# Rope tables beside w_out, operand parts freed tile by tile, norm columns inside blocks and out of the banks' turn

## The reference, cut to what matters

```
u = rmsnorm(x) @ w_in;  y = [pool_mixer(u), ssm_mixer(u)]          # first block
x = x + y @ w_out                                                  # "mix"
x = x + (silu(rmsnorm(x) @ w_gate) * (rmsnorm(x) @ w_up)) @ w_down # "ffn"
x = rmsnorm(x)                                                     # norm_final, end of the first block
cos, sin = rope_tables(positions)                                  # second block
z = rmsnorm(x) @ w_in_2          # "z": latents of q and kv, k_pe, 7 x 256 RWKV columns, then gates
y_a = mla_branch(z, cos, sin);  y_b = rwkv7_branch(z)              # "wkv", "qkv", attention, scan
x = x + (gate_a * y_a + gate_b * y_b) @ w_out_2                    # "mix2"
x = x + square(relu(rmsnorm(x) @ w_ffn_up)) @ w_ffn_down           # "ffn2"
x = x + sigmoid(rmsnorm(x) @ w_ple_gate) * (p @ w_ple_proj)        # "ple"
out = rmsnorm(x)
```

## Time and profile before

| | us |
|---|---|
| median of 3 runs (3169.36 to 3174.61) | 3171.29 |
| the profiled execution, its own time | 3166.37 |
| its span, first to last instruction | 3164.5 |
| TensorE busy in it | 2930.0 |
| VectorE / ScalarE / GpSimd busy | 1429.1 / 752.2 / 388.6 |

### The profile page before, as it was taken

The page is one execution under the profiler, slowest core; times in us unless marked ns, Lnnn a source line. Parts: engine busy times, 40 slices in busy tenths (PEclk is TensorE's granted clock), DMA queues, the critical chain, the costliest instruction groups (busy, mean ns, idle before and its releaser), DMA issues.

```text
span 3164.5 us, 38694 instructions
## 1 busy us (share of the span) xinstructions
PE 2930.0 (93%) x16576; PEld 2391.8 (76%) x16576; DVE 1429.1 (45%) x2068; ACT 752.2 (24%) x1010; POOL 388.6 (12%) x293
## 2 busy tenths in 40 slices
PE   5879899999999999988888879989999999999998
PEld 4757678888888877866667657768878888888876
DVE  6983433332333554434442655674343333333354
ACT  4133211111111321024332423231221111111232
POOL 0000101000010210000000700122221101111221
PEclk7989999999999999999989989889999999999999
DMA  4051011111111123234436321325211111111111
GB/s 153 32 123 40 35 56 49 54 40 54 54 40 54 52 76 111 80 124 127 130 119 176 87 54 55 107 95 186 85 38 52 54 40 54 54 40 54 53 54 54
DMA packets 222442, 236.97 MB, mean 75 GB/s; under 512 B 60256, under 2 KB 174816, under 8 KB 221376
## 3 DMA queue, kind: packets, MB, share of 16 engines
q1 hardware_dynamic: 222272, 234.49, 23.2%
HBM read 178.50 MB, written 56.20 MB: 74 GB/s over the span
## 4 chain that ended last, share of the span: by engine, by line
PE 80%; DVE 12%; ACT 3%; issue 2%; DMA 2%; SPq 1%; POOL 0%; DVEq 0%; ACTq 0%
PE bank L618 19%; PE bank L619 19%; PE bank L620 19%; PE bank L2407 2%; PE bank L1761 2%; PE bank L2427 2%; PE bank L1762 2%; PE bank L1763 1%; PE bank L2605 1%; PE bank L3119 1%; PE bank L3121 1%; PE bank L3120 1%; PE bank L3128 1%; DVE w_lo L182 1%; DVE gates L182 1%
## 5 line engine op out<-in xcount | busy, mean ns | idle before, releaser
L618 PE MATMUL bank<-op_hi,w_hi 128*128 128x512 f32 x1824 | 716.4, 393 | 35.3 <-DVE gates L182 14.4
L619 PE MATMUL bank<-op_lo,w_hi 128*128 128x512 f32 x1824 | 713.9, 391 | 0.0
L620 PE MATMUL bank<-op_hi,w_lo 128*128 128x512 f32 x1824 | 713.6, 391 | 0.0
L618 PEld LDWEIGHTS bank<-op_hi,w_hi 128*128 128x128 f32 x1824 | 345.4, 189 | 111.1 <-issue 31.2
L620 PEld LDWEIGHTS bank<-op_hi,w_lo 128*128 128x128 f32 x1824 | 345.0, 189 | 72.3
L619 PEld LDWEIGHTS bank<-op_lo,w_hi 128*128 128x128 f32 x1824 | 345.4, 189 | 71.4
L182 DVE TENSOR_TENSOR w_lo<-w_raw,w_hi 128x2048 fp32r<-128x2048 f32 (+2 forms) x116 | 256.3, 2210 | 209.0 <-ACT w_hi L423 205.2
L618 PE MATMUL bank<-f_hi,w_hi 128*128 128x512 f32 x864 | 336.7, 390 | 3.2 <-POOL f_lo L182 3.2
L619 PE MATMUL bank<-f_lo,w_hi 128*128 128x512 f32 x864 | 336.8, 390 | 0.0
L620 PE MATMUL bank<-f_hi,w_lo 128*128 128x512 f32 x864 | 336.8, 390 | 0.0
L182 DVE TENSOR_TENSOR hT<-hT,bank 128x512 f32<-128x512 f32 x256 | 169.7, 684 | 326.3 <-PE bank L620 326.0
(11 more groups left out here) (454 smaller groups left out, 3966.4 us busy)
## 6 DMA issues: line engine op xcount, KB each, us to landing
record<-record_scratch SPq DMA_DIRECT2D x16, 1024.0 KB, 5.3
w_raw<-in_w_ffn_up SPq DMA_DIRECT2D x16, 1024.0 KB, 5.2
w_raw<-in_w_ffn_down SPq DMA_DIRECT2D x16, 1024.0 KB, 4.8
w_raw<-in_w_in SPq DMA_DIRECT2D x13, 1024.0 KB, 5.5
w_raw<-in_w_gate SPq DMA_DIRECT2D x11, 1024.0 KB, 4.9
w_raw<-in_w_up SPq DMA_DIRECT2D x11, 1024.0 KB, 5.0
w_raw<-in_w_down SPq DMA_DIRECT2D x10, 1024.0 KB, 4.8
w_raw<-in_w_in SPq DMA_DIRECT2D x17, 512.0 KB, 4.2
```

The costliest lines, as they stand in the source:

```text
L618: t.matmul(ps[:], hi[:, k, wc], x[0][:, k, xc], start=k == 0, stop=False)
L619: t.matmul(ps[:], hi[:, k, wc], x[1][:, (k + turn) % KD, xc], start=False, stop=False)
L620: last = t.matmul(ps[:], lo[:, k, wc], x[0][:, k, xc], start=False, stop=k == kt - 1)
```

## The change

1. `dense` gets an order of its k and a signal `free`: behind the last block of w_out (and of w_out_2) each k counts up, so that ScalarE and VectorE write part k of the next operand while that block still runs. The first block of w_out takes k in the order 4 to 7, 0 to 3. The last two residual tiles and their squares move behind the first parts.
2. The rope tables are computed in w_out's second block; the load of the positions and the two stores move ahead in SP's queue. VectorE's wait for the stores stays where it was.
3. The columns and spreads of norms no longer take a turn of the banks (`ahead`): they use the next ones, and the next block starts at its own.
4. The sum of squares for norm_mix_2 moves from GpSimd to VectorE, and the last tile's squares of both norms are no longer added but multiplied by the ones themselves (32 products instead of 16).
5. The norms of the latents move into the first two RWKV blocks, columns ahead of k = 2 and spread ahead of k = 6.

```diff
-        b = order[self.turn[group] % len(order)]
-        self.turn[group] += 1
+        b = order[(self.turn[group] + (ahead or 0)) % len(order)]
+        self.turn[group] += ahead is None
...
+                if free and j + 4 >= len(jobs):
+                    if n < kt - 1:
+                        last.then_inc(*T.up(free, k))
+                    else:
+                        T.also(free, k)
...
-            ps = tile_of(t, "all", name, half)
+            ps = tile_of(t, "all", name, half, ahead=1 + half)
...
-        ps = tile_of(t, "all", name)
+        ps = tile_of(t, "all", name, ahead=0)
...
     def mix_sync(q):
-        for i in range(5):
+        for i in range(3):
+            wt1.load_at(q, i)
+            if i == 1:
+                q.wait_ge(*Sm.T.of("pooled", 3, 1))
+                q.wait_ge(*Sm.V.of("glu lo", 7, 1))
+                q.dma_start(mem.pos[:], a["positions_2"].to_broadcast([P, L])).then_inc(*d_pos.up(by=16))
+        rope_sync(q)
+        for i in range(3, 5):
             wt1.load_at(q, i)
...
-        s.wait_ge(*wt1.used(B_OUT + 3))
         for k in range(KD):
+            s.wait_ge(*T.of("op", k))
             if k >= 6:
                 s.wait_ge(*Sm.V.of("h", k, 1))
...
-            if k in (2, 3):
-                s.wait_ge(*Sm.V.of("h", k + 4, 1))
-                nm1.square(s, k + 4, hT[:, k + 4, :])
+            if k >= 6:
+                nm1.square(s, k, hT[:, k, :])
...
         for b in range(4):
             wt1.lo_at(v, B_OUT + b)
+            if b == 1:
+                yield from rope_vector(v)
...
         for k in range(KD):
-            if 1 <= k <= 2:
-                yield from residual_vector(v, Sm, "out", hT, (5 + k,), "h")
+            if k == 3:
+                yield from residual_vector(v, Sm, "out", hT, (6, 7), "h")
+            v.wait_ge(*T.of("op", (k + 4) % KD))
...
-    nm_h = Norm("norm_mix_2", Sf, mem.sq, mem.acc, Sf.G)
+    nm_h = Norm("norm_mix_2", Sf, mem.sq, mem.acc, Sf.V)
...
         for n, nm in enumerate((nm_h, nm_x)):
+            t.wait_ge(*Sf.V.of(nm.name, "sum", KD - 2))
+            t.wait_ge(*Sf.A.of(nm.name, "sq", KD - 1))
             for j in range(L // P):
-                last = t.matmul(ps[:, 8 * n + j:8 * n + j + 1], nm.acc[:, j * P:(j + 1) * P], ones[:, 0:1], start=True,
-                                stop=True)
+                for m, x in enumerate((nm.acc, nm.sq[(KD - 1) % 2])):
+                    last = t.matmul(ps[:, 8 * n + j:8 * n + j + 1], x[:, j * P:(j + 1) * P], ones[:, 0:1], start=m == 0,
+                                    stop=m == 1)
...
                     if i > 1:
+                        nm_h.add(v, i - 1)
                         nm_x.add(v, i - 1)
                     yield
-        nm_x.add(v, KD - 1)
...
-        for n in range(1, KD):
-            nm_h.add(g, n)
-            yield
...
+        norm_q = {2: lambda: columns_tensor(t, T, nm_q, "cols q", Sz.G.of("latent_q", "sum", 2)),
+                  6: lambda: spread_tensor(t, T, ncol[:, 0, :], "rs q", Sz.V.of("col q"))}
+        norm_kv = {2: lambda: columns_tensor(t, T, nm_kv, "cols kv", Sz.G.of("latent_kv", "sum", 1)),
+                   6: lambda: spread_tensor(t, T, ncol[:, 0, :], "rs kv", Sz.V.of("col kv"))}
...
         for b, n in enumerate(rwkv_blocks):
-            yield from block(B_RWKV + b, "rwkv", n)
-            if b == 0:
-                columns_tensor(t, T, nm_kv, "cols kv", Sz.G.of("latent_kv", "sum", 1))
-                spread_tensor(t, T, ncol[:, 0, :], "rs kv", Sz.V.of("col kv"))
+            yield from block(B_RWKV + b, "rwkv", n, (norm_q, norm_kv)[b] if b < 2 else None)
```

More of the change, by code:

```diff
@@ L134, in begin, with open @@
         self.turn, self.tenant, self.opened = dict.fromkeys(self.groups, 0), {}, set()
-    def open(self, group, *label):
+    def open(self, group, *label, ahead=None):
         assert label not in self.opened, label
@@ L591, in after, with tile_of @@
                 e.wait_ge(*s.total())
-    def tile_of(t, group, *label):
-        ps = psum.open(group, *label)
+    def tile_of(t, group, *label, ahead=None):
+        ps = psum.open(group, *label, ahead=ahead)
         for w in psum.free(*label):
@@ L602, in landed, with dense @@
             e.wait_ge(*d.total())
-    def dense(t, T, w, i, x, kt, jobs, ready, group="all", turn=0, at=None):
+    def dense(t, T, w, i, x, kt, jobs, ready, group="all", turn=0, at=None, order=None, free=None):
         hi, lo = w.view(w.hi, i), w.view(w.lo, i)
@@ L611, in dense @@
             tiles = [tile_of(t, group, *label) for _, _, label in four]
-            for k in range(kt):
+            for n, k in enumerate(order or range(kt)):
                 if j == 0 and at is not None and k in at:
@@ L617, in dense @@
                 for (wc, xc, label), ps in zip(four, tiles):
-                    t.matmul(ps[:], hi[:, k, wc], x[0][:, k, xc], start=k == 0, stop=False)
+                    t.matmul(ps[:], hi[:, k, wc], x[0][:, k, xc], start=n == 0, stop=False)
                     t.matmul(ps[:], hi[:, k, wc], x[1][:, (k + turn) % KD, xc], start=False, stop=False)
-                    last = t.matmul(ps[:], lo[:, k, wc], x[0][:, k, xc], start=False, stop=k == kt - 1)
-                    if k == kt - 1:
+                    last = t.matmul(ps[:], lo[:, k, wc], x[0][:, k, xc], start=False, stop=n == kt - 1)
+                    if n == kt - 1:
                         last.then_inc(*T.up(*label))
+                if free and j + 4 >= len(jobs):
[3 more added lines that the diff above has]
+                        T.also(free, k)
             yield 11
@@ L1253, in mix_tensor @@
             yield from dense(t, T, wt1, B_OUT + b, op, KD, halves_of([(0, 2 * b), (P, 2 * b + 1)], "out"),
-                             (lambda k: Sm.V.of("pool lo" if k < 4 else "glu lo", k, 1)) if b == 0 else None, turn=4)
+                             (lambda k: Sm.V.of("pool lo" if k < 4 else "glu lo", k, 1)) if b == 0 else None, turn=4,
+                             order=(4, 5, 6, 7, 0, 1, 2, 3) if b == 0 else None, free="op" if b == 3 else None)
     def mix_scalar(s):
@@ L1276, in mix_scalar @@
             wt1.hi_at(s, B_OUT + b)
+            if b == 1:
+                yield from rope_scalar(s)
             for i in (2 * b, 2 * b + 1) if b < 3 else ():
@@ L1420, in norm_h_tensor @@
     def norm_h_tensor(t):
-        ps = tile_of(t, "all", "cols h")
-        t.wait_ge(*Sf.V.of("norm_final", "sum", KD - 1))
-        t.wait_ge(*Sf.G.of("norm_mix_2", "sum", KD - 1))
+        ps = tile_of(t, "all", "cols h", ahead=0)
         for n, nm in enumerate((nm_h, nm_x)):
+            t.wait_ge(*Sf.V.of(nm.name, "sum", KD - 2))
+            t.wait_ge(*Sf.A.of(nm.name, "sq", KD - 1))
             for j in range(L // P):
-                last = t.matmul(ps[:, 8 * n + j:8 * n + j + 1], nm.acc[:, j * P:(j + 1) * P], ones[:, 0:1], start=True,
-                                stop=True)
+                for m, x in enumerate((nm.acc, nm.sq[(KD - 1) % 2])):
+                    last = t.matmul(ps[:, 8 * n + j:8 * n + j + 1], x[:, j * P:(j + 1) * P], ones[:, 0:1], start=m == 0,
+                                    stop=m == 1)
         last.then_inc(*Sf.T.up("cols h"))
@@ L2927, in mix2_vector @@
         for k in range(KD):
-            if 1 <= k <= 2:
-                yield from residual(5 + k)
+            if k == 6:
+                yield from residual(6)
+                yield from residual(7)
             v.wait_ge(*A.of("norm hi", k))
```

21 lines of the change are left out of this document (7 added, 14 removed).

## The result

The changed kernel takes 3131.95 us (median of 4 runs, 3124.95 to 3134.3) where the kernel before takes 3170.32 beside it on the same chip (4 runs, 3167.08 to 3174.61): ratio 0.987, 95% interval 0.9858 to 0.9883. The forecast was 3128.6, in a range of 3117 to 3140. The profiled execution took 3134.3 (span 3132.5), the slowest of the four, against 3166.4 for the one of before: 32.0 between the two profiles, where the sum was 42.7.

The account below looks back on a forecast made before the run. TensorE, busy 93% of the span, was taken as the bound, so only its waits and half-clock stretches could yield time. The terms summed to 42.7 us off the 3171.3 median, giving 3128.6, range 3117 to 3140.

Parts of the forecast that it names:

- Entry to the first FFN: From w_out's last matmul into the gate block: operand parts written while w_out's last block runs, gain 4.5 us.
- Rope and banks: Between gate and up block: the wait for banks and split queued behind rope goes, rope costing nothing elsewhere; gain 16.1 us.
- Entry to ffn2: The parts and bank edits at ffn2, without rope: both losses go, gain 10.9 us (some 3.9 and 6.9).
- Gate tiles: Four gate tiles of z: with norms out of the bank turn, the first one's bank is read in time; gain 4.6 us.
- Order of w_out: w_out's first block in the order 4 to 7, 0 to 3: gives nothing, as four pooled tiles must be read first.
- First latent block: From w_down to this block's end: faster sums on VectorE, 1.3 us wait, 10.7 columns, 1.6 slow matmuls; gain 4.4 us.
- Second and third latent block: In z: the second gains 0.4 us, the third loses 1.5 waiting for banks of the x norm's factors.
- Latent norms inside blocks: First two RWKV blocks: old loss 8.93 us becomes 5.6, including a new 3.7 wait for the lo split; gain 3.3.
- columns at full clock, split in time: Rival in z: columns run at full clock and the latent split is ready; total 3121 us, chance 0.2.
- The new waits in z take it all: Rival: later sums, half-clock columns, second RWKV block's split 3 us later; gain sum 37.3, total 3134 us, chance 0.23.
- The slower case: Rope in SP's queue delays the FFN's first gate load; slower only if tables come later than 373 us; chance 0.02.

Follow-up runs that it names:

- again: The changed kernel with nothing altered, run for a second profile: 3122.15 us, ratio 0.9847 to the kernel before.
- order_plain: Changed kernel with w_out's first block taking its tiles in the order 0 to 7 instead of 4 to 7, 0 to 3: 3130.95 us, ratio 0.9876.
- add_last: Changed kernel with the last squares of both norms added on VectorE, so 32 column instructions instead of 64: 3126.21 us, ratio 0.9855.
- pool_sum: Changed kernel with norm_mix_2's squares summed on GpSimd again and 32 column instructions: 3132.47 us, ratio 0.9877.

## Why the prediction was right

The time lies inside the range, 3.4 above the number. Three sets of runs of this instruction stream (the changed kernel, again, and order_plain, which differs in the order of one block) gave 38, 49 and 40 us less than before; their mean is 42.5, the sum was 42.7. With the three 11 us apart, that the mean comes within 0.2 is luck; that the places add up to 40.8 and 42.5 us in the two profiles of the kernel is not. Step by step:

- **Entry to the first FFN**, 4.5: 4.61.
- **Rope and banks**, 16.1: 16.13; rope cost nothing in its new place. The forecast's reading that the two have one value together was right; how it splits (14.5 and 1.6) I got wrong in an expectation, not in the sum.
- **Entry to ffn2**, 10.9: 10.8, in 3.92 and 6.87. **Gate tiles**, 4.6: 4.6, though TensorE's next wait, for ScalarE's g_rank, was 7.51 and is 8.34 and 7.90, so up to 0.8 of it is given back. **Order of w_out**, 0: 0.
- **First latent block**, 4.4: 3.9 in one profile, 5.5 in the other. The columns came as said in the first (10.8 for 10.7; 9.2 in the second). The wait of 1.3 didn't: VectorE's period is 5.97 and not 6.1, and the first norm's sum is done 14.0 us behind w_down's last matmul, where the working gave 14.8 and the wait more still; 0.3 of a wait is left. The slow matmuls behind cost 3.0, not 1.6, so within this term one error hid another.
- **Second and third latent block**, -1.1: -1.3, with the wait of 1.53 where it was put.
- **Latent norms inside blocks**, 3.3: 2.1 in both profiles. The wait was forecast at 3.7 and is 3.57; the slow clock behind it was put at 1.7 and is 2.7. In add_last and pool_sum, with the same instructions here, it is 1.75 and the two blocks take 56.3 us, 3.1 less than before. So the term isn't plainly mis-sized: what it lacked was a range for the clock's return.
- **Elsewhere**, 0: -8.8 in the first profiled pair. The prediction had no term for it and needed none: in the second profile the spans differ by 43.3 and the edited places by 42.5. But it took the sum to be comparable with one execution's time, which it is only within some 10 us here, since the clock's return behind the long waits of attention and scan moves that stage between 365.5 and 377.4 us.

Of the rivals, "columns at full clock, split in time" fell on both counts. "The new waits in z take it all" had the right queue, but the split was not later and the columns ran at half clock for only part of their time. The slower case had 64 us to go: the tables were stored at 308.7.

The Trainium skill (SBUF — State Buffer, Who interferes with whom) says that a VectorE instruction with two SBUF inputs contends with a GpSimd instruction that reads SBUF, for a port pair that one of them holds at a time. The traces agree: the same 128x1024 addition takes 3.42 beside GpSimd's sums and 1.22 without. Timeline of GpSimd, kernel before, its addition beside the first one of the earlier trace rows:
```profile
1082.89 2.55 POOL L182 TENSOR_TENSOR sq_sum<-sq_sum,sq 128x1024 f32<-128x1024 f32 x1 [3.88 <-ACT sq L460]
```
GpSimd's is done at 1085.44; VectorE's began at 1083.10 and is done at 1086.53, 1.09 us behind it, about what it takes alone.

## What to carry to other kernels

Read a place's loss between two landmarks, less its instructions at the full-clock rate; such terms added up to within 2 us over the eight of this sum. Before pricing a wait that two causes hold up, ask what each leaves if it goes alone, from the rows of that very place. And when a TensorE-bound kernel is profiled once, take the stages with identical instructions first: what they differ by is what one execution can't tell. A term that holds slow clock behind a wait wants a range: here the same place in the same instructions came out at one of two levels: 21.8 or 23.5 us, 26.95 or 27.9, some 41 or 46.9.

## What the runs showed of the hardware

- The granted clock fell from 1.00 to 0.50 while TensorE issued one-column products without a pause: in two profiles of the same kernel some 3 and 5 us into 64 records, with TensorE busy for 2.00 of 2.00 us in the stretch in which it fell, at 1.6 us difference in cost.
- Behind one and the same wait of 14 us the clock came back after 5 to 6 us in one execution and some 19 in another; what decides which was not found. The Trainium skill (TensorE: Matmul & The Clock Gate, What's actually happening) says of a kernel's start that the number of slow matmuls differs from run to run of one kernel; the traces show the same behind a wait in the midst of one, and 6 us of time for it at a single place.
- A 128x512 product of plain f32 operands takes 0.86 us at clock 1.00 (two records, 0.43 from start to start), 3.8 times the 0.2267 of the dense blocks. The Trainium skill (FP8 and Floating Point Precision, TensorE Precision Notes) gives four passes for true FP32, which agrees.
